# A two-layer decoder step on one core: the feed-forward blocks in two phases, with thirds of 384, 384 and 264 tokens

## The reference

```python
def conv_ffn(x, hist, g, w_up, cw, cb, w_down):
    h = rms_norm(x, g)
    u = jnp.einsum('btd,df->btf', h, w_up)          # 1024 -> 2 x 2816
    ext = jnp.concatenate([hist.astype(u.dtype), u], axis=1)
    c = cb + sum(cw[j] * ext[:, j: j + T] for j in range(CONV_W))   # 3 taps over time
    a, b = jnp.split(c, 2, axis=-1)
    out = jnp.einsum('btf,fd->btd', jax.nn.silu(a) * b, w_down)     # 2816 -> 1024
    return out, ext[:, -(CONV_W - 1):]
```

## Time and profile before

| what | value |
|---|---|
| median of three runs | 2479.17 us |
| the profiled execution, and its span | 2472.42 us, 2470.6 us |
| TensorE busy, mean granted clock | 95%, 0.975 |
| VectorE, ScalarE, GpSimd busy | 55%, 27%, 10% |
| matmuls of the feed-forward and the two mixers' products (L324) on the chain that ended last | 62% |
| from HBM, to HBM | 148.80 MB, 38.01 MB |

### The profile page before, as it was taken

How to read it: one execution, slowest core, us unless ns; L and a number is a source line. 1 busy time by engine, 2 the same in 40 slices (tenths; PEclk the granted TensorE clock), 3 DMA queues, 4 the chain that set the end, 5 groups by cost and what they waited for, 6 DMA issues and landing times.

```text
span 2470.6 us, 40518 instructions
## 1 busy us (share of the span) xinstructions
PE 2336.8 (95%) x16130; PEld 2278.0 (92%) x16141; DVE 1362.4 (55%) x2017; ACT 658.0 (27%) x1129; POOL 259.1 (10%) x332
## 2 busy tenths in 40 slices
PE   7999999999999689999996999788999999999996
PEld 7999999999999589999996876588999999999996
DVE  5855555555545553645533775545655555555554
ACT  5422222222122331322211543232222222222222
POOL 1200000000000141533413220120000000000000
PEclk8999999999999889999998999899999999999998
DMA  5111111111110112222222787411111111111102
GB/s 177 43 43 47 38 51 51 42 51 42 51 42 26 50 62 94 78 93 84 70 70 87 243 261 209 162 44 51 47 47 34 51 51 51 42 50 44 43 25 73
DMA packets 164814, 180.50 MB, mean 73 GB/s; under 512 B 8111, under 2 KB 126655, under 8 KB 164450
## 3 DMA queue, kind: packets, MB, share of 16 engines
q1 hardware_dynamic: 164274, 178.66, 23.3%
q10 hardware_dynamic: 440, 0.45, 0.1%
HBM read 148.80 MB, written 38.01 MB: 76 GB/s over the span
## 4 chain that ended last, share of the span: by engine, by line
PE 70%; issue 14%; POOL 6%; DVE 5%; DMA 3%; ACT 1%; SPq 1%; POOLq 0%; DVEq 0%; ACTq 0%
PE ps L324 62%; POOL kn L1189 3%; PE ps L1447 2%; PE ps L1420 1%; POOL sq L1191 1%; POOL kn L1197 1%; PE ps L1431 1%; PE ps L1389 1%; PE ps L1459 1%; PE ps L632 1%; POOL sq L1194 1%; POOL sq L1192 1%; DMA kvt<-kvs 1%; DVE xl L347 1%; DVE rb L867 1%
## 5 line engine op out<-in xcount | busy, mean ns | idle before, releaser
L324 PE MATMUL ps<-xh,wh 128*128 128x344 f32 x2160 | 460.2, 321 | 14.0 <-DVE wl L741 7.1
L324 PE MATMUL ps<-xl,wh 128*128 128x344 f32 x2160 | 458.9, 321 | 0.0
L324 PE MATMUL ps<-xh,wl 128*128 128x344 f32 x2160 | 456.3, 320 | 0.0
L324 PEld LDWEIGHTS ps<-xh,wh 128*128 128x128 f32 x2160 | 363.7, 188 | 16.1 <-DVE wl L741 7.4
L324 PEld LDWEIGHTS ps<-xl,wh 128*128 128x128 f32 x2160 | 366.1, 189 | 0.0
L324 PEld LDWEIGHTS ps<-xh,wl 128*128 128x128 f32 x2160 | 360.2, 188 | 0.0
L736 ACT ACTIVATE wh<-stage 128x1024 fp32r<-128x1024 f32 x132 | 137.3, 1058 | 755.6 <-PE ps L324 755.6
L853 DVE TENSOR_TENSOR x<-x,ps 128x1032 f32<-128x1032 f32 x176 | 216.3, 1229 | 125.5 <-PE ps L324 125.5
L817 DVE TENSOR_TENSOR ub<-ps,rb 128x1032 f32<-128x1032 f32 x44 | 54.3, 1233 | 374.5 <-PE ps L324 374.5
L324 PE MATMUL ps<-gh,wh 128*128 128x344 f32 x1056 | 227.4, 324 | 23.9 <-issue 16.1
L324 PE MATMUL ps<-gl,wh 128*128 128x344 f32 x1056 | 227.3, 324 | 0.0
(11 more groups left out here) (250 smaller groups left out, 3859.6 us busy)
## 6 DMA issues: line engine op xcount, KB each, us to landing
stage<-in_w_up SPq DMA_DIRECT2D x88, 512.0 KB, 3.8
stage<-in_w_down SPq DMA_DIRECT2D x44, 512.0 KB, 3.5
stage<-in_w_kv SPq DMA_DIRECT2D x24, 512.0 KB, 4.4
kvs<-kn SPq DMA_DIRECT2D x48, 256.0 KB, 2.0
kvt<-kvs SPq DMA_DIRECT2D x16, 512.0 KB, 4.6
out_kv_w_prompt<-kvs SPq DMA_DIRECT2D x13, 512.0 KB, 6.7
om<-os_ SPq DMA_DIRECT2D x8, 792.0 KB, 5.7
stage<-in_w_q SPq DMA_DIRECT2D x12, 512.0 KB, 4.4
```

The lines of the kernel that those rows point to most:

```text
L324: mm = pe.matmul(ps[:, bank0 + c, 0:NW], w, m[:, c * NW:(c + 1) * NW], start=(i == 0), stop=(i == len(parts) - 1))
```

## The change

**Two phases.** The block no longer alternates. The up phase runs all 22 f: the same 72 matmuls of 344 columns a slab. The product g of each f goes from `cb` to a DRAM tensor `gs` (`keep`). Then the down phase runs three times over all 22 f, once for each third c of the tokens (384, 384 and 264 columns). For one f it makes 8 x 3 = 24 matmuls, one for each chunk d and each of the three split products, each chunk in its own PSUM bank; all eight banks accumulate over the 22 f, and only then is x added, once for each chunk and third (`add_x`, 24 a layer). The last two f of a third go chunk by chunk.

**Transfers.** For each f and third SP loads the 512 KB of w_down again and the columns of g (192 KB, or 132 KB in the last third) into `graw`; four slots hold weights (`draw`: three of `stage`, and `rb`, whose factors are done with) and g. ACT and DVE split both (`act_down`, `dve_down`): 1024 and 384 or 264 columns. `w_up` uses two slots of `stage`, not three, and the first slab of f = 1 is split inside the loop, not ahead of the norm.

**The first three down steps** are loaded and split during the last up slab. The fourth (n = 3) is issued by SP behind the store of the last g. The tail groups move into the last three f of the up phase; two stand behind the first down matmuls on d = 0 to 5, since the banks of d = 6 and 7 hold them.

**After a third.** In layer 0 its columns are added, squared and split while TensorE begins the next third; ahead of the last third's additions stand all four first weight pieces of the projection. In layer 1 the third's columns are transposed, copied into a `yst` of all rows, and stored by ACT in row tiles of 128 by 256 columns; the sample rows go with the last third.

```diff
--- before.py
+++ after.py
-NB = NF // 2
-LAST = NB - 1
-SLABS = 3 * NF
+THIRDS = ((0, 384), (384, 384), (768, 264))
+DW = 384
...
+        yst = sb("yst", [P, 9, D], F32, r1)
...
-        wh = sb("wh", [P, 3, 1024], F32R, r2)
-        wl = sb("wl", [P, 3, 1024], F32R, r2)
+        whl = sb("whl", [P, 3, 2, 1024], F32R, r2)
...
-        gh = sb("gh", [P, 2, N], F32R, r2)
-        gl = sb("gl", [P, 2, N], F32R, r2)
+        graw = sb("graw", [P, 4, DW], F32, r2)
+        gdh = sb("gdh", [P, 4, DW], F32R, r2)
+        gdl = sb("gdl", [P, 4, DW], F32R, r2)
+        wx = sb("wx", [P, 2, 1024], F32R, r2)
...
+        draw = (stage[:, 2, :], stage[:, 0, :], stage[:, 1, :], rb[:, 0:1024])
+        wdh = (wh[:, 2, :], wx[:, 0, :], wh[:, 0, :], wh[:, 1, :])
...
+        gs = nc.dram_tensor("gs", [DEPTH, NF, P, N], F32, kind="Internal").ap()
...
+            def up(f, half):
+                sp.dma_start(stage[:, half, :].rearrange("p (k n) -> p k n", k=KC), up_src(L, half, f)).then_inc(f_up_in[half], 16)
+
+            def keep(f):
+                sp.wait_ge(S.prod, f + 1)
+                sp.dma_start(gs[L, bass.ds(f, 1)].rearrange("o p n -> p (o n)"), cb[:, :]).then_inc(S.kept, 16)
+
+            def down(c, f, q, n, k=None):
+                slot = down_slot(c, f if k is None else k)
+                if k is not None or n >= 4:
+                    sp.wait_ge(f_dl, S.dl + 2 * n - 6)
+                elif n == 3:
+                    sp.wait_ge(S.A, NF)
+                    sp.wait_ge(S.B, NF)
+                elif n:
+                    sp.wait_ge(f_lo, S.lo + 2 * NF - 2 + n)
+                if c == 0:
+                    sp.wait_ge(S.kept, 16 * f + 16)
+                sp.dma_start(draw[slot], a["w_down"][L][bass.ds(f * P, P), :]).then_inc(f_wd_in[slot], 16)
+                sp.dma_start(graw[:, slot, 0:THIRDS[c][1]], third(gs[L, bass.ds(f, 1)], c).rearrange(
+                    "o p n -> p (o n)")).then_inc(f_wd_in[slot], 16)
+
+            begin(sp, 0)
+            up(0, 0)
+            begin(sp, 1)
+            up(0, 1)
+            with sp.Fori(1, NF) as f:
+                for half in range(2):
+                    sp.wait_ge(f_lo, S.lo + 2 * f + (half - 1))
+                    up(f, half)
+                keep(f - 1)
+            for f in range(3):
+                down(0, f, 0, f)
+            keep(NF - 1)
+            down_loop(sp, 0, down, 3)
+            for c in range(1, NC):
+                down_loop(sp, c, down)
...
-            with pe.Fori(0, LAST) as j:
-                ups(j)
-                pe_up(pe, S, slot_of(2), 6 * j + 4, 0, (S.A, 6 * j + 2))
-                pe_up(pe, S, slot_of(3), 6 * j + 5, 1, (S.B, 6 * j + 3))
-                pe_down(pe, S, j, (slot_of(4), slot_of(5)), 6 * j + 8, 6 * j + 3, 6 * j + 4)
...
+            for f in range(NF - 3, NF):
+                for half in range(2):
+                    pe_up(pe, S, f, half, (S.B if half else S.A, f))
+                    pe_conv_tails(pe, S, TAILS.get((f, half), ()))
+
+        def pe_down(pe, L, S):
+            def one(c, f, d, slot):
+                w, wt = wdh[slot][:, d * P:(d + 1) * P], wdl[slot][:, d * P:(d + 1) * P]
+                n = THIRDS[c][1]
+                for i, (wt_, m) in enumerate(three(w, wt, gdh[:, slot, 0:n], gdl[:, slot, 0:n])):
+                    mm = pe.matmul(ps[:, d, 0:n], wt_, m, start=(f == 0 and i == 0), stop=(f == NF - 1 and i == 2))
+                return mm
...
+            def free(c, d):
+                if c == 0:
+                    if d < 6:
+                        pe.wait_ge(*((S.A, NF) if d < 3 else (S.B, NF)))
+                    else:
+                        pe.wait_ge(f_ct, S.ct + NF // 2)
+                elif L == 0:
+                    pe.wait_ge(f_xa, S.xa + KC * (c - 1) + d + 1)
+                else:
+                    result_copied(pe, c - 1, d)
...
+            for c in range(NC):
+                if c == 0:
+
+                    for f, ds in ((0, range(6)), (1, range(6)), (0, range(6, KC)), (1, range(6, KC))):
+                        if ds[0] == 0:
+                            ready(f)
+                        elif f == 0:
+                            pe_conv_tails(pe, S, TAILS[NF, 0])
+                        for d in ds:
+                            if f == 0:
+                                free(0, d)
+                            mm = one(0, f, d, down_slot(0, f))
+                        if ds[0] == 6:
+                            mm.then_inc(f_dn, 1)
+                    for f in range(2, 4):
+                        step(0, f, 0, f)
+                else:
+                    for f in range(4):
+                        step(c, f, 0, NF * c + f)
+                with pe.Fori(1, (NF - 2) // 4) as i:
+                    for k in range(4):
+                        step(c, 4 * i + k, 0, 4 * i + (NF * c + k), k)
+                for f in range(NF - 2, NF):
+                    ready(NF * c + f)
+                for d in range(KC):
+                    for f in range(NF - 2, NF):
+                        mm = one(c, f, d, down_slot(c, f))
+                    mm.then_inc(f_fin, 1)
+                    if L == 1 and d >= 2:
+                        pe_result(pe, c, d - 2)
+                if L == 1:
+                    for d in range(KC - 2, KC):
+                        pe_result(pe, c, d)
...
-                steps = conv_steps(v, L, S, 2 * j + 2)
-                for d in range(KC):
-                    add_x(v, S, d, 8 * j + d + 2)
-                    if d < len(steps):
-                        steps[d]()
...
+                    dve_slab(v, S, f + 1, 0)
+                else:
+                    for n in range(3):
+                        dve_down(v, S, 0, n, 0, n)
+                keep_tail(v, S, ua, 0, f)
+                evac(v, S, ub, 1, f)
+                if not last:
+                    dve_slab(v, S, f + 1, 1)
+                keep_tail(v, S, ub, 1, f)
+                conv_steps(v, L, S, f)
...
+        def add_x(v, S, c, d):
+            v.wait_ge(f_fin, S.fin + KC * c + d + 1)
+            nc.vector.tensor_tensor(third(x[:, d, :], c), third(x[:, d, :], c), ps[:, d, 0:THIRDS[c][1]], ALU.add).then_inc(f_xa, 1)
...
+            def split_thirds(c):
+                if c == NC - 1:
+                    first_pieces(act, True)
+                for d in range(KC):
+                    act_split_third(act, ffn[0], split[1], c, d)
+            for c in range(NC):
+                down_steps(act, ffn[0], act_down, c, 3 if c == 0 else 2)
+                split_thirds(c)
             act_project(act)
             act_attention(act)
             act_merge(act)
             act_ffn(act, 1, ffn[1], [])
-            act_conv_tails(act, 1, ffn[1], range(NF // 2))
-            for d in range(KC):
-                copy_result(act, d, 0)
+            for c in range(NC):
+                down_steps(act, ffn[1], act_down, c, 3 if c == 0 else 2)
+                for d in range(0, KC, 2):
+                    copy_result(act, c, d)
+                    if d:
+                        store_result(act, c, d - 1)
+                store_result(act, c, KC - 1)
...
+            for c in range(NC):
+                down_steps(v, ffn[0], dve_down, c, 3 if c == 0 else 2)
+                if c == NC - 1:
+                    first_pieces(v, False)
+                for d in range(KC):
+                    add_x(v, ffn[0], c, d)
+                    if d:
+                        dve_split_third(v, split[1], c, d - 1)
+                dve_split_third(v, split[1], c, KC - 1)
```

607 lines of the change are left out of this document (293 added, 314 removed).

## The result

On the chip the changed kernel takes 2435.18 us (median of 4 runs, 2431.53 to 2440.85), the kernel before 2478.14 us (4 runs there, 2477.01 to 2481.41). Five later runs of the changed kernel gave 2436.54 us (2431.8 to 2439.62) against 2476.16 us, ratio 0.9841 (0.9825 to 0.9856).

A forecast was written before the change was run, and what follows sets the result against it. TensorE was taken to bound the kernel, with gains only at the two blocks' ends: 21.6 + 10.3 - 2.5 = 29.4 us off the 2479.2 us median, 2449.8, forecast as 2449 us, range 2434 to 2468.

The forecast's parts named there:

- Matmuls: Down phase: as many matmuls and columns as before, 176.3 ns for 384 columns and 121.2 ns for 264, so 0 us.
- Rival D: Down matmuls: one matmul per weight is dearer, 9 ns on 3168 matmuls take the whole gain, 2478 us; chance 0.04.
- Keeping pace: Up and down phases: ScalarE's and VectorE's splits and evacuations fit beside TensorE's matmuls, so 0 us.
- Transfers: Down phase: loads at 170 and 227 GB/s stay under some 300 to 314 GB/s, so 0 us.
- From up to down: From U, the last up matmul's end, to step n = 3: 4.8 us waiting plus 2 us for half clock, 6.8 us a layer.
- Third boundaries: Between thirds of the down phase: TensorE's slack about used up, 2 us lost in layer 0, 1 us in layer 1.
- End of layer 0: Projection's second tile starts 17.5 us after E, the last down matmul; layer 0's total 26.3 us, 21.6 us gained.
- End of layer 1: After layer 1's last down matmul: addition, transposes, copies, last store, 6 us; layer 1's total 13.8 us, 10.3 us gained.
- Start of each block: Third up slab: its split now stands behind the evacuation, 1.22 us more, 2.5 us for two layers.
- Rival C: Block ends: no clock fall at n = 3, product at U + 8.1, boundaries free, projection at E + 13: 2436 us; chance 0.12.
- Rival B: Block ends: new waits replace those removed, with full VectorE-GpSimd exclusion, late n = 3, projection at E + 21: 2466 us; chance 0.17.

The follow-up runs named there:

- experiment 3: Changed kernel with one extra 512 KB DRAM-to-DRAM copy issued by SP with each down step's loads: 2441.04 us.
- Experiment 6: Changed kernel with the loads of step n = 3 issued ahead of the store of the layer's last product, not behind it: 2429.95 us.
- experiment 1: Changed kernel with all of layer 0's splits of x and squares made after the last third, not spread over the thirds: 2452.05 us.
- experiments 8 and 9: Changed kernel with two (8) or three (9) of the four projection pieces ahead of the last third's additions, not all four: 2431.13 and 2434.9 us.
- experiment 2: Changed kernel with all of layer 1's result stores issued by ScalarE after the last third, not spread over the thirds: 2446.13 us.
- quarters: Changed kernel with four down passes of 256, 256, 256 and 264 columns, not three; two projection pieces wait for the last down matmul: 2455.68 us.

## Why the prediction was right, and where it was off

The direction and the place were right: everything came from the two ends of the blocks, nothing from the additions that were taken off VectorE in the up phase. The size, 29.4 of 40.9 us, was not, and that the time still lies in the range, 1.2 us above its lower end, owes something to luck. Step by step:

- **Matmuls, 0 us.** Right; 175.9 and 120.9 ns, 0.6 us a layer below my prices. Rival D is refuted with it.
- **Keeping pace, 0 us.** Right. In 104.86:526.50 TensorE is busy for 421.64 us of as many, and VectorE's longer list after the evacuation hides behind the next half.
- **Transfers, 0 us.** Right, with far more room than I had seen: no loss from the loads at 328 and 351 GB/s (experiment 3). The loads of 192 and 132 KB were no harm.
The Trainium skill, DMA: Bandwidth & Descriptors, "Bandwidth", by whose table I had estimated steps of the last third 0.2 us too long: the trace doesn't bear that out, since no step waited for its load at 228 GB/s.
- **From up to down, 6.8 us a layer.** The largest miss: 2.8 us in layer 0 and 3.5 us in layer 1, so 7.3 us too much. The chain of waits there shows why:

```profile
593.29 1.24 DVE cb L936
...
594.55 0.35 SPq L734
...
595.01 0.37 SPq L747
...
595.42 4.51 DMA graw<-gs
...
602.19 0.56 DVE gdl L983
```

The product ended at U + 8.1 (I had put it at 9.2 for ScalarE's taps, which were not late): 1.1 us. From there to the load's landing it took 5.4 us (6.0; the product g is 528 KB, not the 541 I had written, which changes nothing): 0.6 us. The splits and handing over took 2.9 us (3.2): 0.3 us. And no clock fell: 2 us. That makes the 4.0 us of layer 0; in layer 1 the load took 5.22 us and not 4.51. The clock and the product were inside their bounds, but I had chosen the dear side each time, and they add. Experiment 6 confirms the order of events that I gave: the wait for n = 3 is the load behind the store.
- **Third boundaries, 3 us.** The term for layer 0, 2 us, was 1.3 us: n = 3 to E takes 237.8 us, and 236.6 us without the splits (experiment 1). All of it lies at the second boundary. "The slack is about used up" was right: at the first boundary the last addition ends within 0.1 us of the moment at which TensorE needs it. A chunk of 384 columns took 1.29 us, the lower end of my 1.3 to 1.9. At 264 columns one comes every 0.96 us, where whole exclusion of the two engines would make it 0.33 + 0.33 + 0.75 = 1.41 us. GpSimd's addition ran from 848.78 to 849.53, beside VectorE's addition (848.79), and held back only the split behind it: 0.69 us and not 0.43.
The Trainium skill, SBUF — State Buffer, "Who interferes with whom", says that a VectorE operation with at most one SBUF input, outside its two-port modes, doesn't contend with GpSimd. The trace agrees: the addition with one input from PSUM (x<-x,ps) lasted 0.41 us beside GpSimd and 0.76 us for two without it. I had read that rule and still let the upper bound have it for the whole chunk.
- **End of layer 0, E + 17.5.** E + 15.8, with the first addition at E + 5.6 against E + 6.6. The mechanism was right: experiments 8 and 9 show the pieces and sums taking each other's place.
- **End of layer 1, 6 us.** 4.9 us; experiment 2 shows what stood there without the spread stores.
- **Start of each block, 1.2 us.** Right: [2.40] against 1.27 us, 1.15 us each.

The sum: layer 0 gained 28.7 us against 21.6, layer 1 16.3 against 10.3 (each within some 0.3 us, since the transposes moved into the up phase are taken at one price). What is left over of the 40.9 us is a loss of 4.1 us elsewhere, 1.6 more than forecast: the block starts are not it (2.3 us for the two against 2.5), but the stretch from the projection's second tile to layer 1's third slab, 825.4 us against 822.4 (884.10 to 1706.48), of which only 1.15 us are the slab; single executions differ by more there. 7.1 + 6.0 - 1.6 = 11.5 us, the whole difference.

Rival C (0.12, at 2436 us) is what happened in the main: no clock fall, the product at U + 8.1, one boundary of layer 0 free; but the other cost 1.3 us, and its projection at E + 13 was too early. It was not another mechanism but the sum of my own lower bounds. Rival B's condition (full exclusion, everything on one VectorE list) did not arise.

The gain by parts, as the runs have it: 17.5 us of layer 0's from the splits spread over the thirds (16.2 with what comes back at the boundaries), 10.7 us of layer 1's from the stores spread. Each is the loss when that part alone is undone, and they need not add up; if they do, some 13 us of 40.9 are left. I put them down to what the narrower last third shortens, additions and product waits that were 1032 columns wide; no run undoes that part, so it is not shown.

## What to carry to other kernels

An engine's tail behind a matmul phase can be paid inside that phase if the output is finished in pieces along the free dimension. How narrow the pieces may be is set by the follow-up work on all banks together, with whatever stands ahead of it in VectorE's list, against the time until TensorE needs the last bank again: 1.9 + 9.1 us against 11.1 us cost nothing, 1.8 + 9.1 against 9.9 and 2.1 + 6.7 against 7.5 cost 1.4 to 1.5 us each. The work of one bank alone is not the measure: here VectorE was the slower one (1.29 against 1.06 us) even where nothing was lost. Where several estimates on one chain each have room on both sides, choosing the dear side every time adds up to a biased sum: forecast the chain once from the rows' own durations, and keep the bounds for the range. And where loads are to be the bound, find the queues' real limit by adding traffic, not from a busy share.

## Unexpected of the hardware

- A DMA share of 0.83 at 261 GB/s did not mean a limit of 314 GB/s: the same queues moved 328 and 351 GB/s at 0.89, and 408 GB/s at about 1.00. For stores alone it was 319 GB/s at 0.97 (experiment 2). The share is no straight gauge from one kind of traffic to another; why it isn't I haven't tested.
- Idles of 1.5 and 1.1 us at the start of the down phase left the clock at 1.00, those of 2.7 and 2.9 us at the same place in the kernel with quarters had 0.90 over 17.3 us. Behind the 6.01 us idle the projection ran at 0.21 us a matmul and not 0.12 until 850.8, at the level of 1.2 GHz:

```profile
846.80:850.80 4.00, 3.99 (x19) 4.00 (x20) 3.54 (x9) 3.35 (x10) 2.37 (x4) 0.50 0.66 222
```

- In quarters a down matmul of 256 columns took 118.6 ns and one of 264 columns 121.8 ns, where the changed kernel has 120.1 ns for 264 and the projection of the kernel before 117.5 ns for 256. So it is no cost of the width, and its cause is open; the DMA share, 0.72 in quarters' last pass (795:850) and 0.68 in the last third here (790:829), hardly differs.
